# Weight and x loads of two token mixers cut into pieces and set between crossbar transposes, in an eight-core hybrid decoder kernel

## The reference, cut to what matters

```python
for i in range(DEPTH):                       # 2 layers
    h = rmsnorm(x, norm_mix_g[i])
    if i % N_MIXERS == 0:
        x = x + mlstm_mixer(h, ...)          # q,k,v,o,gates = h @ w_in; recurrence; (o * h~ normed) @ w_out
    else:
        x = x + gla_mixer(h, ...)            # q,k,v,r,z = h @ w_in; recurrence; (r * o normed) @ w_out
    h = rmsnorm(x, norm_ffn_g[i])
    x = x + sq_relu_mlp(h, ffn_w1[i], ffn_w2[i])
return rmsnorm(x, final_norm_g)
```

## Time and profile before

| | |
|---|---|
| median of 3 runs | 1527.75 us (1526.99 to 1530.54) |
| the profiled execution | 1532.38 us |
| its span on core 7, the slowest | 1531.1 us |
| spans of all cores | 1518.5 to 1531.1 us |
| TensorE busy | 1435.0 us, 94% |
| VectorE, ScalarE, GpSimd busy | 52%, 36%, 14% |
| granted TensorE clock, mean, core 7 | 0.977 |
| chain that ended last | TensorE 83%, DMA 9%, VectorE 3% |

### The profile page before, as it was taken

How to read it: one execution, slowest core, us unless ns; L and a number is a source line. 1 busy time by engine, 2 the same in 40 slices (tenths; PEclk the granted TensorE clock), 3 DMA queues, 4 the chain that set the end, 5 groups by cost and what they waited for, 6 DMA issues and landing times.

```text
span 1531.1 us, 22634 instructions; the slowest of 8 cores (1518.5 to 1531.1 us)
## 1 busy us (share of the span) xinstructions
PE 1435.0 (94%) x7281; PEld 674.8 (44%) x7281; DVE 795.3 (52%) x1470; ACT 544.0 (36%) x1197; POOL 221.6 (14%) x220
## 2 busy tenths in 40 slices
PE   6959997979999999999999999976999999999997
PEld 2524453434444444444444445432444444444445
DVE  2458382856434434434566877665644343343456
ACT  2546564524013013023256655653420310310335
POOL 5020210412000000000122101133200000000045
PEclk9979999989999999999999999998999999999999
DMA  9863113363330330331101411147330330200015
GB/s 161 208 128 70 19 31 55 59 98 55 55 56 0 56 59 2 55 56 20 36 18 39 114 25 29 14 79 124 56 56 0 55 56 8 48 0 1 1 44 178
DMA packets 85699, 85.26 MB, mean 56 GB/s; under 512 B 52384, under 2 KB 55632, under 8 KB 85584
## 3 DMA queue, kind: packets, MB, share of 16 engines
q0 software_dynamic: 28096, 62.03, 22.1%
q1 hardware_dynamic: 56400, 21.27, 6.9%
q10 hardware_dynamic: 1088, 0.52, 0.1%
HBM read 109.35 MB, written 8.39 MB: 77 GB/s over the span
## 4 chain that ended last, share of the span: by engine, by line
PE 83%; DMA 9%; DVE 3%; issue 2%; POOL 1%; ACT 1%; SPq 0%; ACTq 0%; DVEq 0%; POOLq 0%
PE ps L257 83%; DMA wo<-m_win 3%; DMA ktok_65<-kT 3%; DMA xn_47<-hn 1%; DMA xn_45<-hn 1%; DVE NB L725 0%; DMA ktok_65<-kx_109 0%; DVE hn L271 0%; DVE Cbf L848 0%; DVE R_73 L271 0%; POOL wv L213 0%; POOL xT L213 0%; POOL wqk L213 0%; ACT junk L263 0%; DVE xT L267 0%
## 5 line engine op out<-in xcount | busy, mean ns | idle before, releaser
L263 ACT ACTIVATE rt<-ps 128x512 f32<-128x512 f32 x256 | 152.8, 597 | 620.3 <-PE ps L257 605.3
L267 DVE TENSOR_TENSOR xT<-ps,xT 128x512 f32<-128x512 f32 (+2 forms) x336 | 222.7, 664 | 265.3 <-PE ps L257 264.8
L267 DVE TENSOR_TENSOR hid<-rt 128x512 bf16<-128x512 f32 x240 | 171.5, 717 | 226.9 <-ACT rt L263 226.8
L257 PE MATMUL ps<-hid,w2b_60 128*128 128x512 bf16 x1024 | 221.7, 379 | 0.0
L257 PE MATMUL ps<-hid,w2b_61 128*128 128x512 bf16 (+2 forms) x1024 | 196.4, 352 | 0.0
L257 PEld LDWEIGHTS ps<-hid,w2b_60 128*128 128x128 bf16 x1024 | 100.2, 98 | 120.8
L257 PEld LDWEIGHTS ps<-hid,w2b_61 128*128 128x128 bf16 x1024 | 95.6, 98 | 99.3
L267 POOL TENSOR_TENSOR sd<-sd,sq 128x512 f32<-128x512 f32 x85 | 108.7, 1279 | 83.2 <-ACT sq L263 65.1
L263 ACT ACTIVATE sq<-xT 128x512 f32<-128x512 f32 x136 | 84.5, 628 | 88.5 <-DVE xT L267 56.5
L267 POOL TENSOR_TENSOR sd<-sq 128x512 f32<-128x512 f32 x17 | 21.9, 1290 | 537.9 <-ACT sq L263 490.1
L271 DVE SCALAR_TENSOR_TENSOR R_73<-R_73,egs,ps 128x256 f32<-128x256 f32 x112 | 52.8, 472 | 40.2 <-PE ps L257 38.7
(11 more groups left out here) (225 smaller groups left out, 1882.5 us busy)
## 6 DMA issues: line engine op xcount, KB each, us to landing
w1b_58<-w POOLq DMA_DIRECT2D x8, 1024.0 KB, 12.5
w2b_60<-w POOLq DMA_DIRECT2D x8, 1024.0 KB, 12.7
w1b_59<-w POOLq DMA_DIRECT2D x8, 1024.0 KB, 17.7
w2b_61<-w POOLq DMA_DIRECT2D x8, 1024.0 KB, 11.8
xT<-xT POOLq DMA_DIRECT2D x2, 2048.0 KB, 33.2
wst_110<-m_wout POOLq DMA_DIRECT2D x8, 512.0 KB, 7.6
wst_113<-g_wout POOLq DMA_DIRECT2D x8, 512.0 KB, 4.2
outT<-oT_52 SPq DMA_DIRECT2D x8, 512.0 KB, 3.5
```

The source lines that it names most:

```text
L257: t.op("pe", lambda e: e.matmul(out, lhsT=lhsT, rhs=rhs, start=start, stop=stop), r=r, w=w, sig=sig, ns=max(cols, 64) * (1.7 if f32 else 0 ...
L263: t.op("act", lambda e: e.activation(out=out, in_=in_, func=func, **kw), r=r, w=w, ns=190 + 0.84 * n + (80 if acc is not None else 0))
L267: t.op(eng, lambda e: e.tensor_tensor(out=out, in0=in0, in1=in1, op=op), r=r, w=w, ns=170 + 1.03 * n if eng == "dve" else 200 + 2.2 * n)
```

## The change

Three groups of loads move. wout of layer 0 has four staging buffers, in the tokens of `xT` that belong to group 3 and are not yet loaded; blocks 0 to 3 stand at the start, ahead of the x of group 2, and blocks 4 to 7 go out on SP's queue in chunks 1 and 2. x of group 3 follows on SP's queue in four pieces, in chunks 4 to 7. The first block of w1 goes in pieces in chunks 12, 13 and 14 and the rest at 15, each with `gate` as a read: buffers that transposes write, so that GpSimd waits for these before it issues the load. `ogx` moves to a slot of xn, as the staging was there before. `KX` is written in up to two chunks ahead. In layer 1, wout's loads are hooked one chunk earlier. In chunk 4 the v projections come before the output projections. The planner's cost of DMA is changed: a transpose pays per packet while loads are under way.

```diff
@@ order
             if u["dma"] and u["xp"]:
                 free[e] = st + 1300
-                done[n] = st + 3500
+                pk = 64 if u["xp"] == "hn" else 32
+                b = max(st + 1000, xq)
+                slow = min(pk, int(max(0.0, hbm - b) / 200))
+                xq = b + slow * 200 + (pk - slow) * 18
+                done[n] = xq + 950
             elif u["dma"]:
                 hbm = max(hbm, st + 1500) + u["dma"][1] / 0.29e3
-                done[n] = hbm + (1200 if st < 60000 else 4000)
+                done[n] = hbm + (1200 if st < 60000 else 2500)
@@ build
-    ogx = [at("ogx%d" % i, [128, H * DV], F32, W[3] + 8192 + 4096 * i)[0] for i in range(2)]
+    ogx = [at("ogx%d" % i, [128, H * DV], F32, XO + 2 * SB + 4096 * i)[0] for i in range(2)]
-        wst.append(at("wst%d" % L, [128, 2, D], F32, o2)[0])
+    wst = [[xT[:, 2 * i:2 * i + 2, 3 * GS:] for i in range(4)],
+           [at("wst%d" % i, [128, 2, GS], F32, XO + i * 4096)[0][:] for i in range(2)]]
-    def load_w1(layer, q):
+    def load_w1(layer, q, k0s=(0, 4), n=4, gate=()):
...
-        for k0 in (0, 4):
-            t.dma("pool", [(w1b[s_][:, k0:k0 + 4, :], v[:, k0:k0 + 4, q * 1024:(q + 1) * 1024])], 2097152,
-                  w=[("w1", s_, k) for k in range(k0, k0 + 4)])
+        for k0 in k0s:
+            t.dma("pool", [(w1b[s_][:, k0:k0 + n, :], v[:, k0:k0 + n, q * 1024:(q + 1) * 1024])], n * 524288,
+                  r=gate, w=[("w1", s_, k) for k in range(k0, k0 + n)])
-    def wout_load(layer, k):
+    def wout_load(layer, k, q):
-        i = k % 2
-        t.dma("pool", [(wst[layer][:, i, :], v[:, k, :])], 524288, w=[("wst", layer, i)])
+        i = k % len(wst[layer])
+        halves = lambda ap: ap.rearrange("p (a n) -> p a n", n=GS)
+        t.dma(q, [(wst[layer][i], halves(v[:, k, :]))], 524288, w=[("wst", layer, i)])
@@ Mixer
+        def gate(s, i):
+            return [("hnT", slot(s.layer, (i - 1) // 4), (i - 1) % 4)] + [("ktok", (i + 1) % 2)] * (i < NCH - 2)
+        def ahead(s, i):
+            return i % 4 < 2 or i < 4 and (i == 3 or s.m)
-            return o + ops + v + extra.get(i, [])
+            return o + v + ops + extra.get(i, []) if g == 1 and c == 0 else o + ops + v + extra.get(i, [])
@@ run
-                if not late:
-                    s.KX(i + 1)
+                for fn in ex.pop(-1, []):
+                    fn()
                 s.S2(i)
...
                 s.Cst(i)
+                if s.ahead(i):
+                    s.KX(i + 2)
                 f()
...
-                if late:
-                    s.KX(i + 1)
+                for n in (i + 1, i + 2) if late else (i + 2,) if i == 2 and not s.m else ():
+                    s.KX(n)
@@ start
     t.dma("pool", [(ong[:], ong_d)], 8000, w=[("ong",)])
+    for k in range(4):
+        wout_load(0, k, "pool")
     load_x("pool", 2, 0, 8)
...
     m0.KX(0)
+    m0.KX(1)
@@ ffn_start
-        add(12, (0,), [lambda: load_w1(layer, 0)])
-        add(15, (0, 2), [lambda: load_w2(layer, 0), lambda: load_w1(layer, 1)])
+        mx, last = mix[layer], [("hnT", slot(layer, 3), 3)]
+        for i, k0s in ((12, (0, 2)), (13, (4,)), (14, (6,))):
+            add(i, (-1,), [lambda i=i, k0s=k0s: load_w1(layer, 0, k0s, 2, mx.gate(i))])
+        add(15, (0, 2), [lambda: load_w2(layer, 0, last), lambda: load_w1(layer, 1, gate=last)])
@@ layer 0, layer 1
-    for i, ks in ((0, (0, 1)), (1, (2, 3)), (3, (4, 5, 6, 7))):
-        hooks.setdefault(i, []).extend((n, lambda k=k: wout_load(0, k)) for n, k in enumerate(ks))
-    hooks.setdefault(1, []).extend([(3, lambda: load_x("pool", 3, 0, 8))])
+    for k in range(KC):
+        if k >= 4:
+            hooks.setdefault(k // 2 - 1, []).append((0, lambda k=k: wout_load(0, k, "sp")))
+    for k in range(0, KC, 2):
+        hooks.setdefault(4 + k // 2, []).append((0, lambda k=k: load_x("sp", 3, k, 2)))
-        hooks.setdefault(2 + k // 6, []).append((k % 6, lambda k=k: wout_load(1, k)))
+        i, n = ((1, 11 + k), (2, k - 2), (3, k - 5))[(k > 1) + (k > 4)]
+        hooks.setdefault(i, []).append((n, lambda k=k: wout_load(1, k, "pool")))
```

More of the change, by code:

```diff
@@ L111, in order @@
         free = {e: 1500.0 for e in s.E}
-        done, seq, hbm = {}, [], 0.0
+        done, seq, hbm, xq = {}, [], 0.0, 0.0
         best = {e: None for e in s.E}
@@ L282, in at @@
         return nc.alloc_sbuf_tensor_at(name, list(shape), dt, offset=off), off
-    xT, _ = at("xT", [128, KC, T], F32)
+    xT, XT = at("xT", [128, KC, T], F32)
     PAD = 224
@@ L360, in by_c @@
         return ap.rearrange("p (c n) -> p c n", n=CH)
-    qx, kx, wst = [], [], []
+    wst = [[xT[:, 2 * i:2 * i + 2, 3 * GS:] for i in range(4)],
+           [at("wst%d" % i, [128, 2, GS], F32, XO + i * 4096)[0][:] for i in range(2)]]
+    for i in range(4):
+        for k in range(2 * i, 2 * i + 2):
+            t.reg(("wst", 0, i), XT + k * 8192 + 6144, 2048)
+            t.reg(("xT", k, 3), XT + k * 8192 + 6144, 2048)
+    for i in range(2):
+        t.reg(("wst", 1, i), XO + i * 4096, 4096)
+    qx, kx = [], []
     for L in range(2):
@@ L366, in build @@
         kx.append(at("kx%d" % L, [128, 4, H, CH], BF16, o3 + 4096)[0])
-        o2 = XO + slot(L, 2) * SB
-        wst.append(at("wst%d" % L, [128, 2, D], F32, o2)[0])
-        for i in range(2):
-            t.reg(("wst", L, i), o2 + i * 4096, 4096)
         for h in range(H):
@@ L406, in build @@
             t.reg(("og", p, vb), M + 24576 + p * 4096 + vb * 2048, 2048)
-            t.reg(("og", 2 + p, vb), W[3] + 8192 + p * 4096 + vb * 2048, 2048)
+            t.reg(("og", 2 + p, vb), XO + 2 * SB + p * 4096 + vb * 2048, 2048)
         t.reg(("EB", p), RT + p * 2048, 2048)
@@ L449, in load_cols, with load_w2 @@
                   step * 524288, w=[(nm, hf, k) for hf in range(2) for k in range(k0, k0 + step)])
-    def load_w1(layer, q):
+    def load_w1(layer, q, k0s=(0, 4), n=4, gate=()):
         s_ = q % 2
         v = w1_d[layer].rearrange("(k p) n -> p k n", p=128)
-        for k0 in (0, 4):
-            t.dma("pool", [(w1b[s_][:, k0:k0 + 4, :], v[:, k0:k0 + 4, q * 1024:(q + 1) * 1024])], 2097152,
-                  w=[("w1", s_, k) for k in range(k0, k0 + 4)])
-    def load_w2(layer, q):
+        for k0 in k0s:
+            t.dma("pool", [(w1b[s_][:, k0:k0 + n, :], v[:, k0:k0 + n, q * 1024:(q + 1) * 1024])], n * 524288,
+                  r=gate, w=[("w1", s_, k) for k in range(k0, k0 + n)])
+    def load_w2(layer, q, gate=()):
         s_ = q % 2
@@ L462, in load_w2 @@
             t.dma("pool", [(w2b[s_][:, k0:k0 + 4, :], v[:, k0:k0 + 4, :])], 2097152,
-                  w=[("w2", s_, k) for k in range(k0, k0 + 4)])
-    def wout_load(layer, k):
+                  r=gate, w=[("w2", s_, k) for k in range(k0, k0 + 4)])
+    def wout_load(layer, k, q):
         v = (m_wout_d if layer == 0 else g_wout_d).rearrange("(k p) n -> p k n", p=128)
-        i = k % 2
-        t.dma("pool", [(wst[layer][:, i, :], v[:, k, :])], 524288, w=[("wst", layer, i)])
+        i = k % len(wst[layer])
+        halves = lambda ap: ap.rearrange("p (a n) -> p a n", n=GS)
+        t.dma(q, [(wst[layer][i], halves(v[:, k, :]))], 524288, w=[("wst", layer, i)])
         t.op("dve", lambda e: e.tensor_scalar(
-            out=wout[:, k, :], in0=wst[layer][:, i, :], scalar1=ong[:, layer * 8 + k:layer * 8 + k + 1],
+            out=halves(wout[:, k, :]), in0=wst[layer][i], scalar1=ong[:, layer * 8 + k:layer * 8 + k + 1],
             scalar2=None, op0=ALU.mult), r=[("wst", layer, i), ("ong",)], w=[("wout", k)], ns=750)
@@ L1162, in build @@
     m1.KX(0)
+    m1.KX(1)
     for fn in m1.o(0) + m1.v(1):
```

## The result

The changed kernel takes 1468.8 us (median of 4 runs, 1468.2 to 1469.4) against 1528.0 before: ratio 0.961, 95% interval 0.9593 to 0.9627. The forecast was 1469.0 in a range of 1458 to 1490. The number was right; two of its terms were not, as the experiments show. Some executions on all eight cores run with one die at a lower granted clock and take several per cent longer; the ratios here are from executions without that.

The account below looks back on a forecast made before the run. TensorE bounds the kernel, held at six places by slow transposes: 57.4 us plus 14 of slow clock, 71, less 9.5 charged, gains 61.5; between 1466.3 and 1470.9, forecast 1469 us, range 1458 to 1490.

Parts of the forecast that it names:

- the six holes: Six TensorE stops in both layers' mixers, blamed on slow DMA transposes: 57.4 us, with slow clock after them 71 us.
- A: Layer 0, near 80 us: 17.12 us hole from a transpose beside GpSimd's 2 MB x load; 3 us charged as remaining.
- B: Layer 0's early chunks: 2.92 us hole, transpose beside a 512 KB block from GpSimd; about 1 us charged as remaining.
- C: Layer 0, chunk 12: 9.78 us hole, K transpose behind GpSimd's 4 MB of w1; 1.5 us charged as remaining.
- E: Layer 1's repeat of C: 5.86 us hole from the w1 load; 1 us charged as remaining.
- hidden: FFN norm's sums of squares behind waiting w1 loads: first comes 20 us after chunk 12's gate can open, so no cost.
- the gap suffices, narrowly: Chunk 12 to 13: 2 MB of w1 flow 6.2 us, about 259 to 266, before the next hn transpose near 268.
- D: End of layer 0's mixer: 9.66 us hole, hn transpose slowed by w2 and w1's second block; 1.5 us charged as remaining.
- F: Layer 1's repeat of D at its mixer's end: 12.03 us hole; 1.5 us charged as remaining.
- Collisions: Rival: moved loads still meet transposes, half of 14 at 3.5 us each, 24 us, giving 1493; chance 0.10.
- SP's queue did not become the bound: Rival judged: in chunks 1 to 7 SP loads delay transposes, 90 us over forecast, giving 1559; chance 0.03.
- VectorE as the bound of chunks 12 to 15: Rival: part of TensorE's waiting there was due to busy VectorE anyway, 23 us, giving 1492; chance 0.08.

Follow-up runs that it names:

- the undoings with the old costs: Changed kernel with the planner's old DMA costs, one load group put back each time: start 0.9726, first w1 block 0.9706, chunk 15 loads 0.9759 of the kernel before.

## Why the prediction was right, and where it was not

**The bound and the six holes: right.** That transposes made slow by GpSimd's loads held TensorE, and that the whole price was some 71 us, is what the undoings with the old costs confirm: 65 us for holes that the forecast put at 71 before charges. One reading was off by one: of the six pieces in the earlier trace rows five, not four, stand between 11.30 and 20.99 us; no sum rests on that. The half clock behind each hole went with the holes; the mean granted clock rose from 0.977 on the core profiled before to 0.993 to 0.997 on the eight cores after.

**The start (A, B): right in direction, the charge in the wrong place.** I charged 3 us to A for the tail of the start's loads; there was none, the first hn transpose at 78 and the K transpose behind it were clean. What is left came in chunks 2 to 5: waits of 0.2 to 1.0 us between 92 and 124, 3.8 together, where the kernel before had B's 2.92 and 0.73. One of them hangs on the SP loads as the chain shows: 0.84 us behind VectorE, which is in order and stood before a block of output weights that had not landed:

```profile
108.27 0.75 DVE L480 TENSOR_SCALAR wout<-xT,ong 128x1024 bf16<-128x1024 f32 x1 [1.48 <-DMA xT<-m_wout]
```

The forecast had SP wait for VectorE at these blocks, not VectorE for the load.

**w1 in pieces (C, E): the wrong step.** The forecast said of the sums queued behind a waiting load "hidden", from a row of the sums 20 us after the gate of chunk 12. It looked at one gate. At the gate of chunk 13 GpSimd stood 7.19 us with sums behind it; C, charged with 1.5 us, cost 4.5 and 1.8 of half clock on core 0. Ahead of that "the gap suffices, narrowly" had failed: the forecast took 6.2 us for the 2 MB and 13 from chunk 13's K transpose to the next hn transpose. Chunk 13's K transpose took 4.2 us to land instead of 2.6, the two loads landed 8.3 and 10.2 us after their issue, and the hn transpose went out 10.5 us after that K transpose, with both loads still under way; it took 7.3 us, and the K transpose behind it 6.26. The forecast had priced such a meeting ("about 5 us each"), but as TensorE's wait for the transpose, not as GpSimd's.

**w2 behind the mixer (D, F): right.** A charge of 1.5 us each stands against 0.66 us after D, and about 3 us in small waits over chunks 13 to 15 of layer 1. The late weights cost nothing: from 288.68 TensorE runs through without a break in the chain to 749.6, and no wait for w1 or w2 is among its waits.

**The planner: the missed term.** The forecast gave the new costs 2.9 us either way, since no row priced them. Alone they win 31 us, and beside the loads' new places nothing: there the kernel is, by 3.5 us, probably better without them. The sum came out right because it had been made from the holes, which can be removed only once; the places alone win 63 us, the costs alone 31, both together 60.

**The sum.** Gain 61.5 us against 59.2 by the medians. Charges of 9.5 us stand against some 14 us of holes and half clock after (4.5 and 1.8 in chunk 13, 3.8 at the start, 0.7 and 3.0 at the ends of the mixers), part of which the kernel before had as well. That the forecast met the time to 0.2 us is luck: the charge for C was a quarter of what it cost, the planner's term was taken as nothing, and 2.7 us came from setting the forecast between the median and the profiled execution.

**The signs.** Of the signs of being right, TensorE's waits for ktok (1.2 us in all) and VectorE's for hn transposes (none) came out. Three did not in full: a transpose of 6.26 us is on the chain, the granted clock is 0.79 and 0.87 from 250 to 270 us, and the 2 MB of w1's first two issues ran into the next transposes.

**The rivals.** Collisions happened, as single transposes of 5 to 7 us, at a cost of a few us and not 24. SP's queue did not become the bound: its loads landed in 6.3 and 5.7 us in the median instead of the 3.5 taken, and no transpose is late by them for more than 0.9 us of TensorE's time. VectorE as the bound of chunks 12 to 15 was not seen in the changed kernel beyond waits of a us or less, apart from the hole that starts at GpSimd.

**The rule.** The Trainium skill, "DMA: Bandwidth & Descriptors", section "Issuing engines are not separate DMA queues", has the DMAs of SP, ScalarE and GpSimd share the 16 engines and interleave. The runs agree as far as they go: eight loads of SP's, moved to GpSimd's queue and so to another time, cost 5.7 us with a K transpose of 9.87 us. Behind the same transposes on GpSimd's queue they still cost some 4.6 us, which the rule does not explain and which is not settled. Pieces without gates were as bad as one load.

## What to carry to other kernels

Where a short transfer on the critical path shares the DMA engines with bulk loads, it is first the time of the bulk load that counts: gate it on the short transfer's landing. How much may then go out at once depends on the room before the next short transfer: 8 MB behind a mixer's last transpose cost nothing that was seen, while 2 MB in chunk 12 still met the next two. Cutting a load without setting its time gained nothing, and what the queue is worth was not settled. A gate on an in-order engine holds everything behind it, so check each gate, not the first, for what stands behind it and who waits for that. Telling a list scheduler what contention costs and removing the contention are two remedies for the same holes: measure them apart, since undoing either one alone understates it.

## What the runs showed that I had not expected

One K transpose was slow with no load of GpSimd's near. In the changed kernel SP issues the K transpose of chunk 6 and, 1.4 us later, a 512 KB piece of x:

```profile
116.41 1.27 SPq L218 DMA_TRANSPOSE ktok_65<-kx_111  x1
117.78 0.53 SPq L218 DMA_DIRECT2D xT<-xT  x1
```

The transpose took 5.16 us (chain above); in the kernel before, at the same place and without a load, it took 3.7. That a load slows the transpose issued ahead of it on the same queue does not follow. One chunk later the same order stands, with the piece of x 1.3 us behind the K transpose:

```profile
128.31 1.22 SPq L218 DMA_TRANSPOSE ktok_66<-kx_111  x1
129.62 0.54 SPq L218 DMA_DIRECT2D xT<-xT  x1
```

and that transpose landed after 2.4 us, on the other cores after 2.4 to 2.5:

```profile
DMA to landing us min/median/max: 2.4/2.4/2.4
```

What slowed the transpose of chunk 6 is open. It cost TensorE 0.33 us.

The planner's new cost of a transpose, made to follow the loads, did not make the kernel with well-placed loads faster, but, by 3.5 us, probably slower.
